# Reordering three mixers on one core: banded attention with its operand rounded from the accumulator, and latent scores moved in front of a transpose

## The reference

```python
# first block, twice (l = 0, 1)
proj = h @ w_in[l]
o_a = silu(layer_norm(depthwise_conv(a * sigmoid(g))))           # branch a, 31 taps
o_b = blocked_attention(q, k, v, HEAD_DIM ** -0.5)                # 4 heads of 64
o_c = u * (sgu_w @ layer_norm(sv) + sgu_b)                        # branch c
o_d = blocked_attention(q_full, k_full, v_d, 96 ** -0.5)          # 4 latent heads
mix = concatenate([o_a, o_b, o_c, o_d]) @ w_out[l]

# second block, odd layer: banded attention with sinks
qkv = h @ wqkv + bqkv                                             # 16 query heads, 4 key heads of 64
s = where(mask, q @ k.T / 8 - slope * dist, -inf)                 # window of 128
p = softmax(concatenate([s, sink]))[..., :-1]
x = x + (p @ v) @ wo + bo
```

## Time and profile before

| | |
|---|---|
| median of 3 runs (lowest, highest) | 1894.81 us (1890.09, 1895.89) |
| the profiled execution, its own time | 1892.0 us |
| span of its instructions | 1890.2 us |
| PE busy | 96% of the span |
| DVE, ACT busy | 66%, 48% |
| mean granted clock of TensorE | 0.991 |

### The profile page before, as it was taken

How to read it: one execution, slowest core, us unless ns; L and a number is a source line. 1 busy time by engine, 2 the same in 40 slices (tenths; PEclk the granted TensorE clock), 3 DMA queues, 4 the chain that set the end, 5 groups by cost and what they waited for, 6 DMA issues and landing times.

```text
span 1890.2 us, 31322 instructions
## 1 busy us (share of the span) xinstructions
PE 1821.7 (96%) x12542; PEld 1661.7 (88%) x12555; DVE 1245.2 (66%) x1556; ACT 902.4 (48%) x1086; POOL 72.9 (4%) x69
## 2 busy tenths in 40 slices
PE   6999999999999999999999999999999998999999
PEld 6986999997799989998988889999999986879998
DVE  5788867788886676556665646555655568455555
ACT  5555544445644444334545445333533367554332
POOL 0000200000200000000060000000000000000000
PEclk9999999999999999999899999999999998999999
DMA  9624655542455536554533635555555532335553
GB/s 311 195 74 150 201 188 189 170 137 89 156 201 200 185 129 200 181 192 138 158 112 134 225 110 165 191 178 188 179 181 193 182 134 78 130 105 175 181 184 126
DMA packets 231748, 311.75 MB, mean 165 GB/s; under 512 B 11894, under 2 KB 204310, under 8 KB 231030
## 3 DMA queue, kind: packets, MB, share of 16 engines
q1 hardware_dynamic: 228678, 298.07, 47.4%
q0 software_dynamic: 2704, 10.91, 1.8%
q10 hardware_dynamic: 288, 1.69, 0.2%
HBM read 307.50 MB, written 3.15 MB: 164 GB/s over the span
## 4 chain that ended last, share of the span: by engine, by line
PE 91%; ACT 4%; DVE 4%; issue 1%; DMA 0%; ACTq 0%; DVEq 0%
PE bank L694 48%; PE bank L954 19%; PE bank L850 7%; PE bank L703 4%; PE bank L717 4%; PE bank L750 1%; ACT w_hi L1570 1%; DVE w_lo L2164 1%; DVE x L2161 1%; PE bank L996 1%; PE bank L1020 1%; PE bank L1139 1%; PE bank L1128 0%; DVE bn L2252 0%; PE bank L1318 0%
## 5 line engine op out<-in xcount | busy, mean ns | idle before, releaser
L2164 DVE TENSOR_TENSOR w_lo<-raw,w_hi 128x2048 fp32r<-128x2048 f32 x280 | 641.9, 2301 | 324.7 <-ACT w_hi L1570 324.2
L1570 ACT ACTIVATE w_hi<-raw 128x2048 fp32r<-128x2048 f32 x280 | 533.0, 1905 | 642.4 <-PE bank L694 418.7
L694 PE MATMUL bank<-xt_hi,w_hi 128*128 128x256 f32 x2544 | 723.0, 284 | 4.9 <-DVE w_lo L2164 3.3
L694 PE MATMUL bank<-xt_lo,w_hi 128*128 128x256 f32 x2544 | 720.7, 283 | 0.0
L694 PE MATMUL bank<-xt_hi,w_lo 128*128 128x256 f32 x2544 | 720.7, 283 | 0.0
L694 PEld LDWEIGHTS bank<-xt_hi,w_hi 128*128 128x128 f32 x2544 | 488.6, 192 | 9.3 <-issue 3.7
L694 PEld LDWEIGHTS bank<-xt_lo,w_hi 128*128 128x128 f32 x2544 | 488.5, 192 | 2.4 <-issue 0.2
L694 PEld LDWEIGHTS bank<-xt_hi,w_lo 128*128 128x128 f32 x2544 | 488.5, 192 | 0.0
L954 PE MATMUL bank<-w_hi,act_hi 128*128 128x512 f32 x528 | 206.6, 391 | 0.0
L954 PE MATMUL bank<-w_lo,act_hi 128*128 128x512 f32 x528 | 206.2, 390 | 0.0
L954 PE MATMUL bank<-w_hi,act_lo 128*128 128x512 f32 x528 | 205.4, 389 | 0.0
(11 more groups left out here) (328 smaller groups left out, 2006.2 us busy)
## 6 DMA issues: line engine op xcount, KB each, us to landing
raw<-in_ffn_wi SPq DMA_DIRECT2D x88, 1024.0 KB, 5.1
raw<-in_ffn_w_up SPq DMA_DIRECT2D x44, 1024.0 KB, 5.1
raw<-in_ffn_wo SPq DMA_DIRECT2D x44, 1024.0 KB, 4.8
raw<-in_ffn_w_down SPq DMA_DIRECT2D x22, 1024.0 KB, 5.4
raw<-in_w_in SPq DMA_DIRECT2D x14, 1024.0 KB, 5.4
raw<-in_ssd_in_proj SPq DMA_DIRECT2D x14, 1024.0 KB, 5.2
raw<-in_mem_wkv SPq DMA_DIRECT2D x9, 1024.0 KB, 8.1
raw<-in_w_out SPq DMA_DIRECT2D x8, 1024.0 KB, 4.9
```

Source lines behind the costliest of these rows:

```text
L694: ins = first(mm(dst, w[s][:, k, c0:c0 + m], xt[v][:, k, :], start=k == 0 and p == 0, stop=k == KT - 1 and p == 2))
L1570: return act.activation(dst, src, ACT.Copy)
L2164: return dve.tensor_tensor(out=out, in0=in0, in1=in1, op=op)
```

## The change

In the mixers PE's `scores(2)` comes ahead of `turn_probs(1)`, `branch_c` comes ahead of `outputs(1)`, and the first and third unit of the output projection are multiplied by halves: first the three matmuls of feature half 0 for all four banks, then those of half 1, each half waiting only for its own pair. `turn_probs(3)` stands behind `mean_a` and a row, and all rows of the second unit stand ahead of `variance_a`. ACT and DVE are reordered to suit: `split` stands ahead of `turned_pair(1)`, and `result(1)` between the two heads of `exponentials(2)`.

In the banded attention `operand` is gone: `result` rounds straight into `act_hi`, and a `low_half` for each pair makes `act_lo` from bank 2 and frees the bank. The value projection stands later (unit order 4, 0, 1, 2, 5, 3), the scores and transposes of the first pairs earlier, the roots of the query norms are taken in three parts instead of two, `outputs(p)` stands between two rows, and the splits of weights are laid at other places, one of them cut in two (`split_half`). The number of matmuls, of exponentials and of split units is the same.

```diff
-QKV_ORDER = (4, 0, 1, 5, 2, 3)
+QKV_ORDER = (4, 0, 1, 2, 5, 3)
...
-    def rows_of(tt, h):
+    def rows_of(tt, h, parts=(0, 1)):
         b = 4 + 2 * tt + h
-        for r in range(2):
+        for r in parts:
             for p, (s, v) in enumerate(PASSES):
...
-    turn_probs(1)
     taken(f"{t}.mk")
     pe.wait_ge(rot_ready, seen.next(rot_ready))
     scores(2)
+    turn_probs(1)
+    branch_c()
     outputs(1)
-    branch_c()
     units = [f"out{l}.{j}" for j in OUT_ORDER]
     out_banks(f"{t}.out")
-    rows_of = out_unit(units, 0, (f"{t}.o0", f"{t}.o1"))
-    rows_of(0, 0)
-    rows_of(0, 1)
+    rows_of = out_unit(units, 0, (f"{t}.o0",))
+    for tt, h in ORDER:
+        rows_of(tt, h, (0,))
+    taken(f"{t}.o1")
+    rows_of(0, 0, (1,))
+    rows_of(0, 1, (1,))
     scores(3)
-    rows_of(1, 0)
-    rows_of(1, 1)
+    rows_of(1, 0, (1,))
+    rows_of(1, 1, (1,))
     turn_probs(2)
     rows_of = out_unit(units, 1)
     rows_of(0, 0)
     rows_of(0, 1)
     outputs(2)
-    turn_probs(3)
     mean_a()
     rows_of(1, 0)
+    turn_probs(3)
+    rows_of(1, 1)
     outputs(3)
     variance_a()
-    rows_of(1, 1)
-    rows_of = out_unit(units, 2, (f"{t}.o2", f"{t}.o3"))
+    rows_of = out_unit(units, 2, (f"{t}.o2",))
     for tt, h in ORDER:
-        rows_of(tt, h)
+        rows_of(tt, h, (0,))
+    taken(f"{t}.o3")
+    for tt, h in ORDER:
+        rows_of(tt, h, (1,))
     finish_rows(f"{t}.out", out_unit(units, 3))
...
-        b, g = (3, 6)[j // 2], j // 2
-        if j % 2 == 0:
-            claim(b, f"wss{g}")
+        b, at0 = (3, 2, 6, 6)[j], 8 if j == 3 else 0
+        if j < 3:
+            claim(b, f"wss{j}")
         for i in range(2):
             for tt in range(TT):
-                at = 8 * (j % 2) + 4 * i + tt
+                at = at0 + 4 * i + tt
                 ins = mm(bank[b][:, at:at + 3:2],
                          w_sq[:, 2 + 2 * (j % 2) + i, P * tt:P * tt + P], cst("mean64")[:, 0:P:64],
                          start=True, stop=True)
-        if j % 2:
+        if j != 2:
...
     square_sums(0)
+    key_copies()
     query_half(w, 7, 1, first).then_inc(bank_full[7], 1)
-    pe.wait_ge(small_in, SMALL_AT["swa"])
-    w, first = weights("qkv5", (KT, 256)), First()
-    claim(6, "wv")
-    values_half(w, 0, first)
-    key_copies()
-    square_sums(1)
-    values_half(w, 1, first).then_inc(bank_full[6], 1)
     for kt in range(2):
         taken(f"wk{kt}")
     scores(0)
     w, first = weights("qkv2", (KT, 256)), First()
     claim(4, "w2")
     query_half(w, 4, 0, first)
+    square_sums(1)
     scores(1)
     query_half(w, 4, 1, first).then_inc(bank_full[4], 1)
-    taken("wv")
+    pe.wait_ge(small_in, SMALL_AT["swa"])
+    w, first = weights("qkv5", (KT, 256)), First()
+    claim(6, "wv")
+    values_half(w, 0, first)
     scores(2)
+    turn_probs(0)
+    values_half(w, 1, first).then_inc(bank_full[6], 1)
     w, first = weights("qkv3", (KT, 256)), First()
     claim(5, "w3")
     query_half(w, 5, 0, first)
-    turn_probs(0)
-    query_half(w, 5, 1, first).then_inc(bank_full[5], 1)
+    taken("wv")
     outputs(0)
     scores(3)
+    turn_probs(1)
+    query_half(w, 5, 1, first).then_inc(bank_full[5], 1)
     square_sums(2)
+    outputs(1)
     square_sums(3)
-    turn_probs(1)
-    outputs(1)
     for p in range(2, SWA_PAIRS):
         if p + 2 < SWA_PAIRS:
             scores(p + 2)
...
         if p == 2:
             out_banks("swa.out")
         if p % 2 == 0:
-            rows_of = out_unit(outs, p // 2 - 1)
-        for h in range(2):
-            rows_of(p % 2, h)
+            rows_of = out_unit(outs, p // 2 - 1, (f"w.o{p - 2}", f"w.o{p - 1}"))
+        rows_of(p % 2, 0)
         outputs(p)
-    finish_rows("swa.out", out_unit(outs, 3))
+        rows_of(p % 2, 1)
+    finish_rows("swa.out", out_unit(outs, 3, ("w.o6", "w.o7")))
...
-    def exponentials(p):
-        act.wait_ge(max_ready, seen.next(max_ready))
-        for i in range(2):
+    def exponentials(p, parts=(0, 1)):
+        if 0 in parts:
+            act.wait_ge(max_ready, seen.next(max_ready))
+        for i in parts:
...
     turned_pair(0)
     exponentials(1)
-    result(0)
     b = full(f"{t}.mq")
     drained(f"{t}.mq", copy(m_qn[:, :, :], b[:, :]))
+    result(0)
     b = full(f"{t}.mk")
     drained(f"{t}.mk", copy(m_kn[:, :, :], b[:, :]))
     b = full(f"{t}.mv")
     drained(f"{t}.mv", copy(m_v[:, :, :], b[:, :]))
     act.wait_ge(var_ready, seen.next(var_ready))
     act.activation(sd[:, 0:TT], mv[:, :, 1], ACT.Sqrt, bias=eps[:, 0:1]).then_inc(sd_ready, 1)
+    split()
     turned_pair(1)
-    split()
+    exponentials(2, (0,))
     result(1)
-    exponentials(2)
+    exponentials(2, (1,))
     exponentials(3)
     turned_pair(2)
...
     def result(p):
         act.wait_ge(even_rows, seen.next(even_rows))
         b = full(f"w.o{p}")
-        drained(f"w.o{p}", copy(mix[:, p, :], b[:, 0:T]))
+        if p >= 4 and p % 2 == 0:
+            act.wait_ge(unit_passed, place[f"swaout{p // 2 - 2}"][0] + 2)
+        copy(act_hi[:, p // 2 % 2, p % 2, :], b[:, 0:T]).then_inc(rounded, 1)
...
     queries(0)
-    split()
-    queries(1)
+    deviations(0)
     split()
     for kt in range(2):
         b = full(f"wk{kt}")
         drained(f"wk{kt}", copy(w_k[:, 2 * kt:2 * kt + 2, :], b[:, :]))
-    deviations(0)
+    queries(1)
+    split()
+    deviations(1)
+    exponentials(0)
+    exponentials(1)
+    queries(2)
+    turned_pair(0)
+    split()
     b = full("wv")
     drained("wv", copy(w_v[:, :, :], b[:, :]))
     split()
-    exponentials(0)
-    queries(2)
-    exponentials(1)
-    for p in range(SWA_PAIRS):
-        if p in (1, 3, 5, 7):
+    result(0)
+    exponentials(2)
+    turned_pair(1)
+    queries(3)
+    result(1)
+    deviations(2)
+    turned_pair(2)
+    exponentials(3)
+    result(2)
+    exponentials(4)
+    for p in range(3, SWA_PAIRS):
+        turned_pair(p)
+        if p in (3, 6):
             split()
-        turned_pair(p)
-        if p == 1:
-            deviations(1)
+        result(p)
+        if p == 6:
+            split()
         if p + 2 < SWA_PAIRS:
             exponentials(p + 2)
-        if p == 0:
-            queries(3)
-        result(p)
     split()
...
+def split_half(i):
+    q = split_next[0]
+    slot, n = split_waits(q)[0], UNIT // 2
+    dve.wait_ge(hi_ready, q + 1)
+    part = slice(n * i, n * i + n)
+    ins = tt_(w_lo[:, q % RING, part], raw[:, slot, part], w_hi[:, q % RING, part].bitcast(F32), ALU.subtract)
+    if i:
+        ins.then_inc(unit_split, 1)
+        split_next[0] += 1
...
     more_taps(23, 1)
+    latent_rope()
+    finish(1)
     low_half(0)
-    finish(1)
-    latent_rope()
+    more_taps(25, 1)
     value_norm()
-    more_taps(25, 1)
     maxima(2)
-    low_half(1)
     gate_c()
     operand(1, "c")
-    split()
+    low_half(1)
     finish(2)
+    split()
...
-    def operand(u):
-        for j in range(2):
-            taken(f"w.o{2 * u + j}")
-        if u >= 2:
-            dve.wait_ge(unit_passed, place[f"swaout{u - 2}"][0] + 2)
-        split_operand(u % 2, mix[:, 2 * u:2 * u + 2, :])
+    def low_half(p):
+        dve.wait_ge(rounded, seen.next(rounded))
+        drained(f"w.o{p}", tt_(act_lo[:, p // 2 % 2, p % 2, :], bank[2][:, 0:T],
+                               act_hi[:, p // 2 % 2, p % 2, :].bitcast(F32), ALU.subtract))
     g, at, _ = prow["attn_bqkv_2"]
     dve.tensor_scalar(w_gained[:, :], par[:, g, at:at + 8], par_col("attn_qnorm_2"), None,
...
     split()
     dve.wait_ge(small_in, SMALL_AT["swa"])
     dve.tensor_scalar(w_sink[:, 1, :], w_sink[:, 0, :], -1.0, None, ALU.mult)
+    key_norm()
+    seen.next(norm_ready)
+    split()
     for tt in range(TT):
         ins = tt_(x[:, tt, :], x[:, tt, :], wide[:, 0, :], ALU.add)
     step(ins)
-    split()
-    key_norm()
-    split()
-    split()
     query_scales(0)
+    split()
     maxima(0)
+    split()
+    query_scales(1)
     maxima(1)
-    seen.next(norm_ready)
-    for p in range(SWA_PAIRS):
+    finish(0)
+    finish(1)
+    maxima(2)
+    split()
+    low_half(0)
+    maxima(3)
+    finish(2)
+    split()
+    low_half(1)
+    query_scales(2)
+    maxima(4)
+    low_half(2)
+    for p in range(3, SWA_PAIRS):
         finish(p)
-        if p in (2, 4, 6):
-            operand(p // 2 - 1)
-        if p == 2:
-            query_scales(1)
         if p + 2 < SWA_PAIRS:
             maxima(p + 2)
-        if p in (0, 1, 3, 5, 7):
+        if p in (4, 5):
+            split_half(p - 4)
+        if p == 7:
             split()
-    operand(3)
+            split()
+        low_half(p)
```

26 lines of the change are left out of this document (14 added, 12 removed).

## The result

| | before | changed |
|---|---|---|
| runs on the same chip | 4 | 4 |
| median (lowest, highest), us | 1894.6 (1890.09, 1895.89) | 1873.5 (1871.78, 1877.8) |
| the profiled execution, us | 1892.0 | 1871.78 |
| its span, us | 1890.2 | 1870.0 |
| its mean granted clock | 0.991 | 0.997 |

The ratio is 0.9901, 95% interval [0.9881, 0.9921]: the change makes the kernel 1.0% faster, 18 to 19 us. In the profiled executions it is 20.2 us.

The account below looks back on a forecast made before the run. PE was taken as the bound, busy 1821.7 of 1890.2 us. 5.2 + 3.4 + 7.6 + 1.7 - 1.7 = 16.2 us off gave 1875.8 from the profiled execution, 1878 from the median; 1877 was named, range 1869 to 1886.

Parts of the forecast that it names:

- the case named likeliest: Whole kernel: as summed, or a little better or worse, 12 to 20 us less, 1872 to 1883; chance 0.58.
- First mixer, 5.2: First mixer: the last unit starts on PE at 172.6 instead of 177.81, 5.2 us earlier.
- Second, 3.4: Second mixer: same order and gain as the first less the difference in clock, 3.4 us.
- Banded attention to `turn_probs(2)`: Banded attention: `turn_probs(2)` starts at 1574.1 instead of 1578.49, without waits of 0.68 and 3.22 and a slow `scores(4)`.
- `turn_probs(3)` at 1581.6 with a wait of 2.3: Banded attention: PE, free at 1579.3, waits 2.3 us for ACT's chain with two table loads, then `low_half(2)` and `finish(3)`.
- The ring, 5.7 us a pair: Banded attention from pair 3: transposes, rows, `outputs`, `result`, `low_half`, `finish` and handovers take 5.7 us a pair, before 6.46.
- The last unit at 1609.4: Banded attention: the last unit starts behind `low_half(7)` and two whole splits, at 1609.4 against 1616.99, 7.6 us earlier.
- -1.7 for a fall at the new wait of 2.3 us: Banded attention, ahead of `turn_probs(3)`: a clock fall, 3.3 us at half speed, taken as likelier than none; costs 1.7 us.
- the third rival: Gain given back to clock falls (mixers, two-column matmuls) and a ring of 6.2; 9.3 us left, 1885; chance 0.15.
- The rival by which the kernel would be slower: Banded attention: `low_half` waits behind ACT's exponentials, ring 8.3, costing 10.4 us; slower from 9.8 a pair; chance 0.04.
- the one that the change does not reach the end: Branch a's chain and the two late splits take all; only the clock's share stays, under 5.7 us; chance 0.06.
- The second: Clock holds at every place and branch a's chain is a little shorter: 20.5 us less, 1872 or 1874; chance 0.17.

Follow-up runs that it names:

- e8: The changed kernel itself run once more, unchanged, in a later group; median 1873.12 us, 0.9896 of the kernel before.
- e5: Changed kernel with the identity in place of the third query root (pairs 4 to 7), so two table loads fall away; 1874.63 us, ratio 0.9906 to before.
- e4: Changed kernel with ACT's `result(p)` behind `exponentials(p+2)` for pairs 3, 4 and 5, as before the change; 1884.55 us, ratio 0.9950 to before.
- e6: Changed kernel in its new order, with the banded attention's operand form of before (`operand`, no `low_half`); 1871.27 us, ratio 0.9888 to before.

## Why the prediction was right, and where it was not

1877 was forecast, 1873.5 measured, inside the range, by the case named likeliest, at its fast edge. (16.2 us under the median of 1894.81 are 1878.6, not 1878; it changes nothing else.) On the basis of the sum, the profiled execution, 16.2 us were forecast and 20.2 came. How near the two are is in part luck: by the other trace of the same kernel (e8, 1880.54 us) only 11.5 would have come. The waits and the lengths of the stretches hang less on it, and the steps are judged by these.

- **First mixer, 5.2: 5.6. Second, 3.4: 3.9.** Right, with their make-up: no wait ahead of `turn_probs(1)`, 0.42 ahead of `outputs(1)` (0.65), 7.07 us of branch a's chain (7.1), a last wait of 1.6 (1.3). What the sum did not say is that only 2.3 of it belongs to the order for certain; the falls of 3.4 and 1.6 us are a throw that the profiled execution of before had lost twice.
- **Banded attention to `turn_probs(2)`.** 1574.1 forecast, 1563.77 + 10.1 = 1573.9 measured.
- **`turn_probs(3)` at 1581.6 with a wait of 2.3.** 1571.24 + 10.1 = 1581.3 with 1.96. Right in time, with one error in the working: both loads of tables were counted on the path, and e5 shows that one is.
- **The ring, 5.7 us a pair.** (1593.64 - 1571.24) / 4 = 5.60. e4 shows ACT's `result` to be in it, and e6 `low_half`. The 6.46 us of before, with which it was compared, were not all ring: the clock was at half there until 1583.5, 5 us into these pairs. The fall had begun at 1573.27 and lasted 10.24 us, and the working had priced only the 0.72 of it that lies on `scores(4)`:

```profile
1573.27:1583.51 10.24, 7.02 (x29) 5.00 (x25) 7.37 (x23) 6.71 (x19) 0.00 (x0) 0.50 0.31 102
```

- **The last unit at 1609.4.** 1598.42 + 10.1 = 1608.5: 8.5 us where 7.6 were forecast. It comes behind `low_half(7)` and two splits, as said, but the wait near 1 us ahead of it did not: PE's last row ends at 1598.30.
- **"The operands' new form costs PE nothing by itself."** Wrong: 1.8 us (e6). The text put `low_half` into the ring and then did not price it against the form of before.
- **+1.7 for the last unit's clock.** Came: from the start of the last unit to that of the next stage are 9.16 us instead of 10.81.
- **-1.7 for a fall at the new wait of 2.3 us.** This step failed. The wait came and no fall began behind it, in none of the eight traces of this order. Where a fall comes there, it begins ahead of the wait, at the narrow matmuls, where the third rival had put it. This is 1.7 of the 4.0 us missed. The others are 0.9 (last unit), 0.8 (mixers) and 0.65 between the stages, where no step was about anything: two falls that before does not have, at 703 and 887 us, and one near 930 that is 3.4 us long instead of 10.2.

The rival by which the kernel would be slower is ruled out by the ring of 5.60, and the one that the change does not reach the end by the starts of the last units, 5.6 and 8.5 us earlier. Of the one that gives the change back to the clock and to ACT, the ring of 6.2 and the falls in the mixers did not come; its fall at the two-column matmuls came in four traces of eight. The second (the clock holds at every place, 20.5 us) fits the number of the profiled execution and half of its make-up: the clock did hold in the three stretches, but branch a's chain is no shorter and the wait of 1.6 us stayed. The runs as a whole, at 18.7, lie between it and the first.

One of the signs of being wrong did show: the clock fell at new places, at 703 and 887 us. They lie outside the change, and the waits ahead of them are the old ones. The kernel before, its timeline and the window behind the wait (columns of the earlier trace rows, clock 1.00):

```profile
711.42 0.39 PE L694 MATMUL bank<-xt_hi,w_hi 128*128 128x256 f32 x1 [3.29 <-DVE w_lo L2164]
```

```profile
711.42:715.00 3.58, 3.58 (x30) 3.58 (x31) 2.88 (x3) 1.72 (x3) 0.00 (x0) 1.00 0.64 200
```

And the changed kernel, with the clock at 0.50:

```profile
701.95 0.39 PE L694 MATMUL bank<-xt_hi,w_hi 128*128 128x256 f32 x1 [3.28 <-DVE w_lo L2185]
```

```profile
702.86:706.27 3.41, 3.41 (x18) 3.41 (x17) 2.68 (x4) 1.55 (x3) 0.00 (x0) 0.50 0.88 296
```

## What to carry to other kernels

Where the cover for a wait is a product that can run now, put it ahead: in each mixer swapping one product with one transpose was worth 2 us, and all the rest of the mixers' rewriting, by difference, 0.3. Follow a ring around all its engines and keep out of it what nobody in it needs (exponentials of a later pair, a subtraction that holds a bank). And before such a gain is credited to an order, take the time at half clock off both sides: here it was half of the whole, and filling the waits with zeros gave 8 us without moving anything.

## What the runs showed of the hardware

Two executions of the same instructions, with the same waits of 1.30 and 0.88 us, ran 7 us at 0.52 in one and at 1.00 in the other. A wait of 3.29 us left the clock at 1.00 in the kernel before, and the same wait, of 3.28 us, was followed by 3.4 us at 0.50 in the changed one. Waits of 1.96 and 2.85 us in the banded attention were not followed by a fall, one of 2.33 was (the transposes at 1585.67 of e4 take 1.54 us instead of 0.87), and a stretch with PE busy without a gap, in which it did matmuls of two columns, was followed by one in four traces of eight. So the code and its waits do not settle whether a given execution has the fall; what does is not shown here. Nor does the mean granted clock hold all of it: two traces of one kernel are 3.0 us apart at their first mixer with a clock of 1.00 shown in both.
